# Attention layers of a four-layer block: the second selection cut into eight steps, its round moved to fourth place, and GpSimd given other weight chunks of q2b

## The chip, the cores and the metric

One core of one Trainium2 chip runs the whole program in one launch. The metric is device time in microseconds (us) of one execution. The kernel before takes 1843.88 us, the median of three runs (1841.74 to 1844.70). A difference of 0.2% is 3.7 us.

## The reference, cut to what matters

Sequence length 256, model width 1024, float32. Layers 0 and 1 (a gated delta rule, retention, pooling and a SwiGLU) are not touched. Layers 2 and 3 are attention layers, and each does this:

```python
(aq, ak, av, iq, ik, iw, bq, bk, bv, cq, ck, cv, gates) = split_columns(u @ w_in)
o_a = dsa_attention(qa, ka, av, iqr, ikr, iw * IDX_HEADS ** -0.5)   # 6 heads, keys chosen by top-k
o_b = dilated_attention(rope(bq), rope(bk), bv)                     # 12 heads in 3 groups
o_c = sink_window_attention(rope(cq), rope(ck), cv, sinks)          # 8 heads
merged = g0 * (o_a @ w_a) + g1 * (o_b @ w_b) + g2 * (o_c @ w_c)
return merged @ w_o
```

Branch a first scores every earlier token with eight small index heads, and each query keeps its 64 best keys:

```python
score = jnp.einsum('bqh,bqhs->bqs', iwb, relu(iq @ ik * idx_scale))
_, idx = lax.top_k(where(causal, score, -inf), 64)
```

## The kernel before, in words

**Weights.** Every projection streams through the core in chunks of 128x1024 float32 (512 KB): 568 of them. SyncE fetches chunk i into one of four slots of `raw` (line 560) as soon as the split of chunk i-4 has freed the slot. ScalarE rounds it to `whi` (line 654) once TensorE has used chunk i-4. VectorE or, for the chunks in the set `SHARED`, GpSimd subtracts to get the rest, `wlo` (lines 1144 and 1800; this is called the split of a chunk). TensorE then does 24 matmuls of 128x256 for a chunk: high weights by high inputs, high by low, low by high (line 2019).

**Order.** There is no scheduler. Each of the five engines has its own Python function that writes its queue in program order, and a generator yields after each chunk. `run(attention(index, attend), fill)` puts the attention pieces between chunks: each `yield 1` of `attention` lets the next chunk of `fill` through. In an attention layer `fill` is q2b (16 chunks, the queries and keys of branches b and c), gate0, gate1 (8 each), wa (3), gate2 (8), wb (2). A chunk of q2b is called by its number below; chunk 16 is the first of gate0. The split of chunk k+3 stands in the step of chunk k.

**Pieces of attention.** `index(half)` gives the scores and the selection for the queries of one half (0 or 1). TensorE does 16 small matmuls, ScalarE a Relu of them, VectorE adds eight weighted heads (line 1150), then does eight selection rounds, each a MAX (line 1662) and a MATCH_REPLACE (line 1664), and two instructions that make the mask. The second half has 256 columns, the first 128. Before the change VectorE does two selection rounds in one step.
`attend(x)` is one of ten rounds: scores on TensorE, mask and maximum on VectorE, exponentials on ScalarE, then transposes, values and a last transpose. A round takes three chunks. The order of the rounds is the list `kinds`; rounds 0 and 1 are branch a for both halves, then come four of b and four of c. Both selections are complete before round 0, which stands before chunk 12. Round t stands before chunk 12+3t.

**Rope.** A pair of q2b tiles is turned in four steps: VectorE evacuates the bank with two multiplications (to `products` for sin, to `QF` for cos) once both chunks of the pair are done; SyncE copies the sin product between partitions with four small DMAs (`exchange`, line 582), which stand in its queue behind the fetch of chunk 2(r-6)+9; GpSimd adds (`rope(r)`, line 1800). The eight pairs of q2b are r = 6 to 13. A round of branch b reads tiles of r = 6 to 11, so TensorE waits in front of the first b round for addition 11. Addition 11 stands in GpSimd's queue behind the split of chunk 17, exchange 11 in SyncE's queue behind the fetch of chunk 19, which waits for the split of chunk 15.

**Banks.** The pairs of q2b alternate between banks 6 and 7, so that chunk 10 needs the evacuation of the pair 6-7 (chunks 6 and 7, r = 9), chunk 12 that of 8-9, and so on.

Of the kernel before, what the change touches and what calls it, by code (L numbers as in the profile page):

```python
# [143 lines left out]
SHARED |= {312 + 138 * L + c for L in (0, 1) for c in chain((1, 2, 3, 8, 9, 10), range(12, 44, 2))}  # L144
# [130 lines left out]
def program(nc, ins, out):  # L275
    with ExitStack() as ctx:
# [251 lines left out]
        kinds = [("a", 0, 0, 3), ("a", 1, 0, 3), ("b", 0, 0, 3), ("b", 0, 1, 3), ("b", 1, 0, 3), ("b", 1, 1, 3),  # L528
# [3 lines left out]
        def attention(index, attend):  # L532

            yield from index(0)
            yield from index(1)
            before = None
            for x in rounds:
                g = attend(x)
                next(g)
                yield 1  # L540
                if before is not None:
                    next(before)
                yield 1
                next(g)
                if before is not None:
                    next(before)
                yield 1
                if before is not None:
                    next(before, None)
                before = g  # L550
            for _ in before:
                yield 1
# [77 lines left out]
        def scalar(a):  # L630
# [347 lines left out]
            def second(L):  # L978
# [37 lines left out]
                def index(half):  # L1016
# [10 lines left out]
                    for _ in range(6):  # L1027
                        yield 1
# [29 lines left out]
                def gates(name, steps, *at):  # L1058

                    for i, s in enumerate(steps):  # L1060
                        yield s
                        if i in at:
# [3 lines left out]
                             gates("wa", after_step(project("gate1", L), 5, lambda: branch_high("wa", L, *a_att.at("OO", L, 1))), 1, 3),  # L1066
# [75 lines left out]
        def vector(v):  # L1142
# [457 lines left out]
            def second(L):  # L1600
# [43 lines left out]
                def index(half):  # L1644
# [5 lines left out]
                    v.wait_ge(*a_att.at("rel", L, half, 1, 4 // (512 // nk) - 1))  # L1650
                    for c in range(2):
                        for j in range(4):
                            at = 8 * half + 2 * j + c
                            x = stt(here, rel[:, c, j, :], IW[:, at:at + 1], here if c + j else causal, OP.mult, OP.add)
                            if c + j < 4:
                                x.then_inc(*v_att.up())
                                v.wait_ge(*v_att.now())
                    x.then_inc(*v_att.up("score", L, half))
                    yield 1
                    for r in range(8):  # L1660
# [5 lines left out]
                        if r % 2:  # L1666
                            yield 1
# [130 lines left out]
        def gpsimd(g):  # L1798
# [156 lines left out]
            def second(L):  # L1955
# [20 lines left out]
                def index(half):  # L1976
                    for _ in range(6):
# [30 lines left out]
        def tensor(e):  # L2008
# [545 lines left out]
            def second(L):  # L2554
# [13 lines left out]
                def index(half):  # L2568
# [14 lines left out]
                    for _ in range(6):  # L2583
                        yield 1

                def attend(x):
# [4 lines left out]
                    if t == 2:  # L2591
# [299 lines left out]
```

## Time and profile before

| what | value |
|---|---|
| median of 3 runs | 1843.88 us |
| the profiled execution's own time | 1846.73 us |
| its span | 1844.9 us |
| TensorE busy | 1805.4 us, 98% |
| VectorE busy | 1250.9 us, 68% |
| ScalarE busy | 952.7 us, 52% |
| GpSimd busy | 315.0 us, 17% |
| granted TensorE clock, mean | 0.997 |

The page gives busy time by engine and by group of instructions. The view of waits lists what an engine waited for, in a stretch, with the total, the number of waits and the longest. A timeline gives for each instruction (or run of like ones, then with their count after the x) its start in us from the start of the span, its duration, engine, line, operation and tiles, and in square brackets the idle time before it and what ended it. When several instructions of one line follow without a pause they share one row, which shows the shape of the first only. "SPq" is the issue of DMAs by SyncE. The two attention layers are the same program; layer 2's attention part runs from 1032 to 1220 us, layer 3's from 1455 to 1650 us, and events of the one stand 423 us behind those of the other until the first wait of TensorE.

### The profile page before, as it was taken

How to read it: one execution, taken by the hardware profiler on the slowest of the kernel's cores; microseconds unless marked ns; L12 is line 12 of the kernel's file. 1: busy time of each engine (PE TensorE's matmuls, PEld its weight loads, DVE VectorE, ACT ScalarE, POOL GpSimd, SP SyncE). 2: the span in 40 equal slices, each digit the busy share in tenths (PEclk: the TensorE clock that was granted, in tenths of full speed). 3: DMA queues.
4: the chain of work that ended last, by engine and by line, in shares of the span. 5: the costliest groups of instructions: out<-in, count | busy, mean ns of one | idle time of the engine just before them, and what ended most of it. 6: DMA issues, size and time to landing. Idle time of an engine off the chain costs nothing.

```text
span 1844.9 us, 37214 instructions
## 1 busy us (share of the span) xinstructions
PE 1805.4 (98%) x15880; PEld 1714.5 (93%) x15880; DVE 1250.9 (68%) x1668; ACT 952.7 (52%) x1377; POOL 315.0 (17%) x174
## 2 busy tenths in 40 slices
PE   7999999999999999999999999999999999999998
PEld 7889998998888999999989999999999889999998
DVE  6885677665689648777648775587647795677643
ACT  5634466544554345564545445556534545556533
POOL 0050231000002303200001453320001352321000
PEclk9999999999999999999999999999999999999999
DMA  6453354656445334655665563456655654445663
GB/s 242 154 167 104 124 174 157 204 193 210 154 149 172 116 115 140 203 177 180 195 196 169 192 206 126 138 178 199 202 191 174 224 188 131 140 168 195 195 196 102
DMA packets 91524, 315.54 MB, mean 171 GB/s; under 512 B 11616, under 2 KB 12768, under 8 KB 91104
## 3 DMA queue, kind: packets, MB, share of 16 engines
q1 hardware_dynamic: 90784, 312.60, 52.3%
q8 instruction: 126, 2.06, 0.5%
q10 hardware_dynamic: 576, 0.57, 0.1%
q14 instruction: 38, 0.31, 0.1%
HBM read 302.90 MB, written 1.05 MB: 165 GB/s over the span
## 4 chain that ended last, share of the span: by engine, by line
PE 84%; DVE 12%; ACT 3%; issue 1%; DMA 0%; SPq 0%; DVEq 0%; ACTq 0%
PE bank L2019 82%; DVE wlo L1144 4%; DVE area L1144 3%; DVE area L1150 2%; ACT area L648 1%; ACT whi L654 1%; PE bank L2613 1%; DVE hl L1150 1%; DVE xT L1150 1%; DMA raw<-in_weights 0%; DVE area L1664 0%; DVE area L1662 0%; PE bank L2634 0%; PE bank L2253 0%; ACT L636 0%
## 5 line engine op out<-in xcount | busy, mean ns | idle before, releaser
L1144 DVE TENSOR_TENSOR wlo<-raw,whi 128x1024 fp32r<-128x1024 f32 x514 | 665.7, 1309 | 388.3 <-ACT whi L654 387.6
L2019 PE MATMUL bank<-hh,whi 128*128 128x256 f32 x2896 | 818.6, 284 | 23.8 <-DVE wlo L1144 18.7
L2019 PE MATMUL bank<-hh,wlo 128*128 128x256 f32 x2906 | 802.1, 277 | 0.0
L2019 PE MATMUL bank<-hl,whi 128*128 128x256 f32 x2896 | 794.4, 278 | 0.0
L654 ACT CAST whi<-raw 128x1024 fp32r<-128x1024 f32 x568 | 585.3, 1047 | 373.3 <-PE bank L2019 324.1
L2019 PEld LDWEIGHTS bank<-hh,whi 128*128 128x128 f32 x2896 | 545.6, 188 | 40.5 <-DVE wlo L1144 23.1
L2019 PEld LDWEIGHTS bank<-hh,wlo 128*128 128x128 f32 x2906 | 546.3, 188 | 0.0
L2019 PEld LDWEIGHTS bank<-hl,whi 128*128 128x128 f32 x2896 | 541.6, 189 | 1.5 <-issue 1.4
L1800 POOL TENSOR_TENSOR area<-area 128x512 f32<-128x512 f32 (+4 forms) x84 | 138.3, 1652 | 535.4 <-ACT area L648 213.3
L1800 POOL TENSOR_TENSOR wlo<-raw,whi 128x1024 fp32r<-128x1024 f32 x54 | 138.4, 2564 | 385.2 <-ACT whi L654 385.2
L2019 PE MATMUL bank<-FH,whi 128*128 128x256 f32 x640 | 177.4, 277 | 0.0
L2019 PE MATMUL bank<-FH,wlo 128*128 128x256 f32 x642 | 176.9, 276 | 0.0
L2019 PE MATMUL bank<-FL,whi 128*128 128x256 f32 x640 | 176.8, 276 | 0.0
L648 ACT ACTIVATE area<-area 128x256 f32<-128x256 f32 (+8 forms) x247 | 140.7, 579 | 50.3 <-DVE area L1144 17.4
L2019 PE MATMUL bank<-area 128*64 128x64 f32 (+6 forms) x2464 | 142.8, 248 | 6.6 <-DVE area L1144 5.2
L2019 PEld LDWEIGHTS bank<-area 128*64 128x64 f32 (+3 forms) x2464 | 122.6, 151 | 24.7 <-issue 7.0
L2019 PEld LDWEIGHTS bank<-FH,whi 128*128 128x128 f32 x640 | 120.2, 188 | 0.4 <-issue 0.3
L2019 PEld LDWEIGHTS bank<-FH,wlo 128*128 128x128 f32 x642 | 120.4, 188 | 0.0
L2019 PEld LDWEIGHTS bank<-FL,whi 128*128 128x128 f32 x640 | 120.2, 188 | 0.1
L1144 DVE TENSOR_TENSOR area<-bank,RSB 128x512 f32<-128x512 f32 (+1 forms) x118 | 80.0, 681 | 30.5 <-PE bank L2019 30.0
L1144 DVE TENSOR_TENSOR area<-bank,area 128x512 f32<-128x512 f32 (+3 forms) x140 | 81.6, 621 | 21.9 <-PE bank L2019 21.3
L2019 PE MATMUL bank<-wlo,FH 128*128 128x512 f32 x240 | 95.1, 396 | 0.0
(132 smaller groups left out, 1905.9 us busy)
## 6 DMA issues: line engine op xcount, KB each, us to landing
raw<-in_weights SPq DMA_DIRECT2D x568, 512.0 KB, 4.1
area<-area SPq DMA_DIRECT2D x100, 64.0 KB, 3.8
area<-area SPq DMA_DIRECT2D x16, 128.0 KB, 4.0
cst<-in_const SPq DMA_DIRECT2D x1, 1188.0 KB, 8.1
cst<-in_const SPq DMA_DIRECT2D x1, 1024.5 KB, 5.8
xT<-in_x SPq DMA_DIRECT2D x4, 256.0 KB, 7.3
out<-xT SPq DMA_DIRECT2D x4, 256.0 KB, 2.8
area<-in_lev SPq DMA_DIRECT2D x2, 384.0 KB, 6.9
```

The lines of the kernel that those rows point to most:

```text
L648: return a.activation(dst, src, fn, scale=scale, **more)
L654: a.copy(whi[:, i % RING, :], raw[:, i % RAW, :]).then_inc(*hi.up(i))
L1144: return v.tensor_tensor(dst, x, y, op)
L1150: return v.scalar_tensor_tensor(out=dst, in0=x, scalar=s, in1=y, op0=op0, op1=op1)
L1800: return g.tensor_tensor(dst, x, y, op)
L2019: return e.matmul(ps, x, y, start=start, stop=stop, skip_group_check=skip)
L2613: o = e.transpose(bank[b][:, 128 * u:128 * u + 128], x.grid()[:, j % 2, j // 2, 128 * kb:128 * kb + 128], C("eye"))
```

## The change

The index and attention parts of layers 2 and 3 are written in another order; no arithmetic changes.

1. The second selection (`index(1)`) is cut. Five of its steps stand before round 0, the others are taken one by one (`next(chosen)`) between the pieces of rounds 0 and 1. On VectorE each of its eight selection rounds has a step of its own, and the eight weighted heads are added in two steps of four, for both halves.
2. Each engine's `index` yields seven times in place of six. `index(1)`'s matmuls stand behind chunk 6 in place of chunk 5. Round 0 still stands before chunk 12.
3. The second round of branch a stands fourth: rounds 1 and 2 are now the first two of branch b. TensorE's wait for rope addition 11 is in front of round 1, and that of ScalarE's wa copy (in step 5 of gate1) is for the output of round 3.
4. Of q2b, GpSimd splits chunks 5, 6, 7, 12, 14 and 15 (before: 4, 5, 6, 11, 12, 13 and 15). From chunk 17 on nothing changes.

```diff
--- before.py
+++ after.py
@@ -141,7 +141,7 @@
 
 SHARED = {146 * L + c for L in (0, 1) for c in (51, 54, 57, 60, 63)}
 
-SHARED |= {312 + 138 * L + c for L in (0, 1) for c in chain((1, 2, 3, 8, 9, 10), range(12, 44, 2))}
+SHARED |= {312 + 138 * L + c for L in (0, 1) for c in chain((2, 3, 4, 9, 11), range(12, 44, 2))}
 
 
 class Signal:
@@ -525,25 +525,30 @@
             def grid(self):
                 return self.scores.rearrange("p (c n t) -> p c n t", c=2, t=self.nk)
 
-        kinds = [("a", 0, 0, 3), ("a", 1, 0, 3), ("b", 0, 0, 3), ("b", 0, 1, 3), ("b", 1, 0, 3), ("b", 1, 1, 3),
+        kinds = [("a", 0, 0, 3), ("b", 0, 0, 3), ("b", 0, 1, 3), ("a", 1, 0, 3), ("b", 1, 0, 3), ("b", 1, 1, 3),
                  ("c", 0, 0, 2), ("c", 0, 1, 2), ("c", 1, 0, 2), ("c", 1, 1, 2)]
         rounds = [Round(i, *x) for i, x in enumerate(kinds)]
 
         def attention(index, attend):
 
             yield from index(0)
-            yield from index(1)
+            chosen = index(1)
+            for _ in range(5):
+                yield next(chosen)
             before = None
             for x in rounds:
                 g = attend(x)
                 next(g)
+                next(chosen, None)
                 yield 1
                 if before is not None:
                     next(before)
+                next(chosen, None)
                 yield 1
                 next(g)
                 if before is not None:
                     next(before)
+                next(chosen, None)
                 yield 1
                 if before is not None:
                     next(before, None)
@@ -1024,7 +1029,7 @@
                             a.wait_ge(*e_att.at("index", L, half, c, k))
                             act(rel[:, c, k * per:k * per + per, :], bank[2 * c + k][:, 0:per * nk].rearrange("p (n t) -> p n t", t=nk), AF.Relu,
                                 scale=0.125 * 8.0 ** -0.5).then_inc(*a_att.up("rel", L, half, c, k))
-                    for _ in range(6):
+                    for _ in range(7):
                         yield 1
 
                 def attend(x):
@@ -1063,7 +1068,7 @@
                             gate(name, L, 2 * at.index(i))
 
                 fill = chain(project("q2b", L), project("gate0", L),
-                             gates("wa", after_step(project("gate1", L), 5, lambda: branch_high("wa", L, *a_att.at("OO", L, 1))), 1, 3),
+                             gates("wa", after_step(project("gate1", L), 5, lambda: branch_high("wa", L, *a_att.at("OO", L, 3))), 1, 3),
                              gates("wb", branch("wa", L), 0, 1),
                              after_step(project("gate2", L), 5, lambda: wb_high()),
                              gates("wc", branch("wb", L), 0, 1))
@@ -1647,23 +1652,24 @@
                     here, there = SC[:, 0:nk], SC[:, 256:256 + nk]
                     causal = C2(f"mA{half}")
                     v.wait_ge(*a_evac.at("v2b", L, 1))
-                    v.wait_ge(*a_att.at("rel", L, half, 1, 4 // (512 // nk) - 1))
                     for c in range(2):
+                        v.wait_ge(*a_att.at("rel", L, half, c, 4 // (512 // nk) - 1))
                         for j in range(4):
                             at = 8 * half + 2 * j + c
                             x = stt(here, rel[:, c, j, :], IW[:, at:at + 1], here if c + j else causal, OP.mult, OP.add)
                             if c + j < 4:
                                 x.then_inc(*v_att.up())
                                 v.wait_ge(*v_att.now())
-                    x.then_inc(*v_att.up("score", L, half))
-                    yield 1
+                        if c:
+                            x.then_inc(*v_att.up("score", L, half))
+                        yield 1
                     for r in range(8):
                         v.wait_ge(*v_att.now())
                         v.max(m8, here).then_inc(*v_att.up())
                         v.wait_ge(*v_att.now())
                         v.match_replace(there, m8, here, TAKEN).then_inc(*v_att.up())
                         here, there = there, here
-                        if r % 2:
+                        if half or r % 2:
                             yield 1
                     am = AM[:, 128 * half:128 * half + nk]
                     v.wait_ge(*v_att.now())
@@ -1974,7 +1980,7 @@
                 rest(after_step(project("v2b", L), 0, lambda: rope(5)))
 
                 def index(half):
-                    for _ in range(6):
+                    for _ in range(7):
                         yield 1
 
                 def attend(x):
@@ -2580,7 +2586,7 @@
                                 x = mm(bank[2 * c + k][:, nk * (j % per):nk * (j % per) + nk], QF3[r, 4 + j, qs], QF3[r, 8, 0:nk], True, True)
                                 if j == k * per + per - 1:
                                     x.then_inc(*e_att.up("index", L, half, c, k))
-                    for _ in range(6):
+                    for _ in range(7):
                         yield 1
 
                 def attend(x):
@@ -2588,7 +2594,7 @@
                     qs = slice(128 * x.half, 128 * x.half + 128)
                     if t == 0:
                         e.wait_ge(s_twin["ak"], 16 * (L - 1))
-                    if t == 2:
+                    if t == 1:
                         e.wait_ge(*g_rope.at("add", L, 11))
                     if t == 6:
                         e.wait_ge(*g_rope.at("add", L, 13))
```

On TensorE in layer 2, in front of the round that now reads q2b's tiles. Before, at chunk 15 (round 1, branch a), and three chunks on (round 2, branch b):

```order
L2019 MATMUL bank<-area 128x256 [waits att_act]
L2019 MATMUL bank<-area 128x256 [waits att_dve] x2
L2019 MATMUL bank<-area 128x256 x2
L2019 MATMUL bank<-area 128x256 [waits att_pe]
L2019 MATMUL bank<-hh,whi 128x256 [waits wlo_pool]
...
L2634 MATMUL bank<-cst,area 128x128 [waits att_act,att_dve]
L2019 MATMUL bank<-area 128x128 [waits att_dve,rope_pool]
```

The changed kernel at chunk 15:

```order
L2025 MATMUL bank<-hh,wlo 128x256
L2025 MATMUL bank<-area 128x128 [waits att_dve,rope_pool]
L2025 MATMUL bank<-area 128x128 [waits att_dve]
L2025 MATMUL bank<-area 128x128 x4
L2025 MATMUL bank<-hh,whi 128x256 [waits wlo_pool]
```

The wait on `rope_pool` (GpSimd's additions) stands three chunks earlier than before. On VectorE, layer 2, from the weighted heads of the second half to its fourth selection round. Before (the pairs MAX, MATCH_REPLACE are selection rounds, `proj` marks the evacuation of a bank, `whi` a split):

```order
L1150 SCALAR_TENSOR_TENSOR area<-area,cst 128x256 [waits att_act,evac_act]
L1150 SCALAR_TENSOR_TENSOR area<-area 128x256 [waits att_dve] x7
L1144 TENSOR_TENSOR wlo<-raw,whi 128x1024 [waits whi]
L1662 MAX area<-area 128x8 [waits att_dve]
L1664 MATCH_REPLACE area<-area 128x256 [waits att_dve]
L1662 MAX area<-area 128x8 [waits att_dve]
L1664 MATCH_REPLACE area<-area 128x256 [waits att_dve]
L1144 TENSOR_TENSOR wlo<-raw,whi 128x1024 [waits whi]
L1144 TENSOR_TENSOR area<-bank,area 128x512 [waits half1,proj]
```

The changed kernel:

```order
L1155 SCALAR_TENSOR_TENSOR area<-area,cst 128x256 [waits att_act,evac_act]
L1155 SCALAR_TENSOR_TENSOR area<-area 128x256 [waits att_dve] x3
L1149 TENSOR_TENSOR wlo<-raw,whi 128x1024 [waits whi,att_dve]
L1149 TENSOR_TENSOR area<-bank,area 128x512 [waits half1,proj]
L1149 TENSOR_TENSOR area<-bank,area 128x512
L1155 SCALAR_TENSOR_TENSOR area<-area 128x256 [waits att_act]
L1155 SCALAR_TENSOR_TENSOR area<-area 128x256 [waits att_dve] x3
L1149 TENSOR_TENSOR wlo<-raw,whi 128x1024 [waits whi]
L1668 MAX area<-area 128x8 [waits att_dve]
L1670 MATCH_REPLACE area<-area 128x256 [waits att_dve]
L1149 TENSOR_TENSOR area<-bank,area 128x512 [waits half2,proj]
```

The evacuation of the pair 6-7 (`half1`) stood behind eight heads and two selection rounds; it now stands behind four heads. On GpSimd, layer 2, from rope addition 7 (`half3`) to addition 9 (`half1`; `wlo` rows are splits). Before, then the changed kernel:

```order
L1800 TENSOR_TENSOR area<-area 128x512 [waits evac_dve,half3]
L1800 TENSOR_TENSOR wlo<-raw,whi 128x1024 [waits whi] x2
L1800 TENSOR_TENSOR area<-area 128x512 [waits evac_dve,half0]
L1800 TENSOR_TENSOR wlo<-raw,whi 128x1024 [waits whi]
L1800 TENSOR_TENSOR area<-area 128x512 [waits evac_dve,half1]
```

```order
L1806 TENSOR_TENSOR area<-area 128x512 [waits evac_dve,half3]
L1806 TENSOR_TENSOR wlo<-raw,whi 128x1024 [waits whi]
L1806 TENSOR_TENSOR area<-area 128x512 [waits evac_dve,half0]
L1806 TENSOR_TENSOR wlo<-raw,whi 128x1024 [waits whi]
L1806 TENSOR_TENSOR area<-area 128x512 [waits evac_dve,half1]
```

The two splits between additions 7 and 8 (chunks 11 and 12) become one (chunk 12), and the next is that of chunk 14 in place of 13.

## Rows read from the trace of the kernel before

**Rows 1.** The page, parts 1 and 5: TensorE whole, VectorE weight subtractions.
```profile
PE 1805.4 (98%) x15880; PEld 1714.5 (93%) x15880; DVE 1250.9 (68%) x1668; ACT 952.7 (52%) x1377; POOL 315.0 (17%) x174
...
L1144 DVE TENSOR_TENSOR wlo<-raw,whi 128x1024 fp32r<-128x1024 f32 x514 | 665.7, 1309 | 388.3 <-ACT whi L654 387.6
```

**Rows 2.** TensorE's waits, 1000:1240: engine, line <- releaser: total, times, longest us.
```profile
PE bank L2019 <- DVE area L1144: 1.1, 1, 1.1
```

**Rows 3.** TensorE's waits, 1420:1660, layer 3's attention.
```profile
PE bank L2019 <- DVE area L1144: 2.5, 2, 1.6
PE bank L2019 <- DVE wlo L1144: 2.0, 1, 2.0
```

**Rows 4.** Windows: length, busy us of PE, PEld, DVE, ACT, POOL, then clock, DMA.
```profile
1040.00:1090.00 50.00, 48.87 (x437) 47.10 (x436) 46.49 (x97) 23.33 (x46) 31.59 (x16) 1.00 0.63 203
1460.00:1515.00 55.00, 50.51 (x448) 48.45 (x447) 53.24 (x98) 22.85 (x41) 30.33 (x15) 1.00 0.54 176
```

**Rows 5.** TensorE timeline (start us, us, instruction): first and last matmul, q2b chunks 0 to 5.
```profile
1456.35 0.38 PE L2019 MATMUL bank<-hh,whi 128*128 128x256 f32 x1
...
1472.68 0.28 PE L2019 MATMUL bank<-hh,wlo 128*128 128x256 f32 x1
```

**Rows 6.** VectorE timeline, layer 2: two selection rounds; evacuation 10; end of round 0.
```profile
1059.55 0.42 DVE L1662 MAX8 area<-area 128x8 f32<-128x256 f32 x1
...
1060.53 0.43 DVE L1662 MAX8 area<-area 128x8 f32<-128x256 f32 x1
...
1075.09 2.21 DVE L1144 TENSOR_TENSOR area<-bank,area 128x512 f32<-128x512 f32 x4
...
1078.31 0.17 DVE L1147 TENSOR_SCALAR area<-area 128x6 f32<-128x6 f32 x1
```

**Rows 7.** VectorE timeline: two operations beside GpSimd ones.
```profile
1094.74 0.95 DVE L1147 TENSOR_SCALAR area<-area 128x2 f32<-128x2 f32 x1
...
1482.05 3.42 DVE L1144 TENSOR_TENSOR wlo<-raw,whi 128x1024 fp32r<-128x1024 f32 x1
```

**Rows 8.** GpSimd timeline, both layers: rope additions (area) and splits (wlo).
```profile
1054.84 1.29 POOL L1800 TENSOR_TENSOR area<-area 128x512 f32<-128x512 f32 x1 [1.82 <-DMA area<-area]
...
1071.45 2.63 POOL L1800 TENSOR_TENSOR wlo<-raw,whi 128x1024 fp32r<-128x1024 f32 x1 [0.91 <-ACT whi L654]
...
1084.32 1.28 POOL L1800 TENSOR_TENSOR area<-area 128x512 f32<-128x512 f32 x1
...
1093.26 2.40 POOL L1800 TENSOR_TENSOR wlo<-raw,whi 128x1024 fp32r<-128x1024 f32 x1 [2.83 <-ACT whi L654]
...
1482.01 2.38 POOL L1800 TENSOR_TENSOR wlo<-raw,whi 128x1024 fp32r<-128x1024 f32 x1 [2.25 <-ACT whi L654]
...
1496.08 1.28 POOL L1800 TENSOR_TENSOR area<-area 128x512 f32<-128x512 f32 x1 [2.02 <-DMA area<-area]
```

**Rows 9.** ScalarE timeline, layer 2: casts of chunk 15 and chunks 17, 18.
```profile
1070.32 1.05 ACT L654 CAST whi<-raw 128x1024 fp32r<-128x1024 f32 x1 [1.78 <-PE bank L2019]
...
1080.85 1.98 ACT L654 CAST whi<-raw 128x1024 fp32r<-128x1024 f32 x2
```

**Rows 10.** TensorE timeline, layer 2: scores of the second round.
```profile
1079.70 1.57 PE L2019 MATMUL bank<-area 64*128 64x256 f32 x12
```

**Rows 11.** SyncE queue's issues: raw is a chunk's weights, area a rope exchange.
```profile
1050.73 2.41 SPq L582 DMA_DIRECT2D area<-area  x4
...
1075.19 0.81 SPq L560 DMA_DIRECT2D raw<-in_weights  x2
...
1489.74 2.41 SPq L582 DMA_DIRECT2D area<-area  x4
```

**Rows 12.** The granted clock: after a 2.58 us pause, and around a 2.0 us one.
```profile
113.03 0.37 PE L2019 MATMUL bank<-area 64*64 64x64 f32 x2 [2.58 <-DVE area L1144]
...
112.00:116.00 4.00, 2.96 (x35) 2.68 (x36) 4.00 (x6) 0.00 (x0) 3.86 (x3) 0.59 0.45 125
1484.00:1488.00 4.00, 2.47 (x21) 2.47 (x22) 3.90 (x8) 0.65 (x1) 3.38 (x2) 1.00 0.31 101
```

## The prediction, written before the changed kernel was run

> **What bounds the kernel now.** I read the page first. TensorE is busy 1805.4 us, 98% of the span [rows 1], so what a change of order can return is TensorE's idle time, not anybody's work. The second view is the list of TensorE's waits in the two attention parts. In layer 2 it names one wait of 1.1 us for VectorE [rows 2], in layer 3 two on an evacuated bank of 2.5 us together and one of 2.0 us on a split [rows 3]. All four lie between chunks 9 and 14 of q2b. The third view, windows, says why: from 1040 to 1090 us VectorE is busy 46.49 of 50 us, in layer 3's stretch 53.24 of 55 [rows 4]. There VectorE is the engine that TensorE waits for. The sum returnable is 1.1 + 2.5 + 2.0 = **5.6 us**, 0.3% of the kernel.
>
> That layer 3 loses four times what layer 2 does, with the same program, is read in the timelines. VectorE's split of 1482.05 took 3.42 us [rows 7] in place of the mean 1.31 [rows 1]; GpSimd had begun a split at 1482.01 that ended at 1484.39 [rows 8], and 1.1 us of work was left then. So where both engines want such an operation, the one that is 40 ns late stands still until the other ends. The Trainium skill says this too (SBUF — State Buffer, Who interferes with whom): DVE operations with two SBUF inputs, and those in a 2-port mode such as a `tensor_scalar`, exclude GpSimd for a whole instruction, while one-input operations outside these modes don't. By that rule the trace agrees: a TENSOR_SCALAR of 2 elements took 0.95 us [rows 7] under a GpSimd split of 1093.26 to 1095.66 [rows 8], where a lone one took 0.17 [rows 6].
>
> **What goes.** A selection round of the second half takes 1060.53 - 1059.55 = 0.98 us [rows 6]. Before chunk 12 VectorE did eight of them, now three; 5 x 0.98 = 4.9 us leave, and the two mask instructions with them. Against that it makes one split more in this stretch, chunk 13 and 11 for 14, 1.3 us [rows 1]. So it is relieved of 3.6 us or more, and the evacuation that chunk 10 waited for stands behind four heads and no selection. VectorE was late by 1.1 us in layer 2 and by 2.0 + 1.6 in layer 3 [rows 2, 3]. I count all 5.6 us as returned. If the collision of layer 3 repeats in a new place some stays: from 0 to 2.0 us. The cover for the selection rounds that now stand beside rounds 0 and 1 is the slack behind chunk 12, where VectorE's next splits are needed a chunk or more later.
>
> **What comes.** TensorE's wait for rope addition 11 moves from round 2 to round 1, three chunks earlier. The chain that leads to addition 11 does not move with it. I take as zero the moment in which ScalarE sees chunk 11 ended, 1070.32 in layer 2 [rows 9]. TensorE then does round 0's scores and chunks 12 to 14, and is in front of round 1 at 1079.70 [rows 10]: **+9.4 us**, in both kernels.
>
> First path, through ScalarE. VectorE evacuates and does round 0's masks and maximum: from 1075.09 to 1078.48, 3.4 us [rows 6]. From there six exponentials, the casts, GpSimd's split of chunk 17 and addition 11, which ends at 1084.32 + 1.28 = 1085.60 [rows 8], take 7.1 us. Sum: +10.5, so **1.1 us late** at the least. With it comes the lock: GpSimd's split of chunk 15 now runs when the maximum's last TENSOR_SCALAR is due, and 0.8 to 1.3 us are added by the measure of the 0.95 us row [rows 7]: +11.3 to +11.8.
>
> Second path, through the queues. The cast of chunk 15 and its split begin at 1071.45 - 1070.32 = +1.1 [rows 8, 9]. But GpSimd must now first do chunk 14's split, which cannot begin before chunk 10's end plus a cast. A chunk is (1472.68 - 1456.35) / 143 x 24 = 2.74 us [rows 5]; so that is -2.7 + 1.1 = -1.6, with 2.4 us of split to +0.8, addition 9 to +2.1, and chunk 15's split to **+4.5** [2.4 and 1.3 us, rows 8]. SyncE then issues one fetch (0.4 us) [rows 11] and exchange 11 at about +5.0. From the issue of an exchange to the addition that waited for it I find 1054.84 - 1050.73 = 4.1 us at the low end and 1496.08 - 1489.74 = 6.3 at the high end [rows 8, 11]. Addition 11 ends between 5.0 + 4.1 + 1.3 = +10.4 and +12.6.
>
> The later of both gives +11.8, typically, if VectorE is in time: a wait of **2.4 us**. If the split of chunk 11 on VectorE falls behind GpSimd's split of chunk 12, which I estimate to begin within half a microsecond of each other (GpSimd's at -3 x 2.74 + 1.1 = -7.1), VectorE is up to 2.4 us late, chunk 15's fetch with it, then addition 9 and all that follows: about 1.6 us more, a wait of **4.0 us**. I give both the same weight and take 3.2 us for each layer, 6.4 us for two, with bounds of 1.1 us (only the first path, no lock) and 5.6 us (slow split and slowest landing) for each. Behind this wait nothing new is late: while TensorE stands, all the others catch up.
>
> **The clock.** Behind a pause of 2.58 us the granted clock was 0.59 over 4 us [rows 12], so about 0.41 x 2 x 4 = 3.3 us at 1.2 GHz. Behind the 2.0 us pause it stayed 1.00 [rows 12]. Dense matmuls in 3.3 us at half clock lose 1.6 us. A wait of 2.4 us may escape this, one of 4.0 hardly; I count one of the two layers, 1.6 us. The Trainium skill (TensorE: Matmul & The Clock Gate, What's actually happening) has the same two levels, with the lower one after idleness; by it, too, a longer pause costs more than its length.
>
> **Other edits.** The wa copy of ScalarE waits for round 3's output, written after chunk 26 and wanted in step 5 of gate1, chunk 29: three chunks of cover, 8 us. The seven yields move `index(1)`'s matmuls one chunk and add none. Two b rounds in front of a's second move work only.
>
> **The sum.** -5.6 + 6.4 + 1.6 = **+2.4 us**. The profiled execution (1846.73 us, 1.8 above its span) stands 2.85 above the median of the runs. I put the change on the median: 1843.9 + 2.4 = **1846.3 us**. It is smaller than the 0.2%, 3.7 us, that a measurement of this kernel can tell from no change.
>
> **Rivals.**
> *The exchange is early and addition 11 in time.* If landings are at their low end and the lock falls well, the wait is under 0.6 us in each layer: -5.6 + 1.2 = -4.4, and at best -5.6, 1838.3 to 1839.5 us. For it speaks that VectorE's relief is surely there; against it that the first path alone needs 10.5 of 9.4 us. Chance 0.18.
> *One long wait in each layer.* Place: TensorE in front of round 1. Price: 5.6 us each and 1.6 us of clock each: -5.6 + 11.2 + 3.2 = +8.8, 1852.7 us. It decides from a wait of about 3.9 us per layer, where with the clock the loss passes 3.7 us (-5.6 + 7.8 + 1.6 = +3.8). For it speaks the near tie between the splits of chunks 11 and 12. Chance of a loss between 3.7 and 8.8: 0.32.
> *The change moves the waits without removing them*, since VectorE loses the race against GpSimd elsewhere: 2.0 us stay, and with waits of 1.1 to 2.4 us the total is -1.4 to +1.2, 1842.5 to 1845.1. It looks like no change. Chance 0.12.
>
> **How the numbers follow.** My forecast, 2.4 to 4.0 us per layer and the clock in none, one or both, spans -5.6 + 4.8 = -0.8 to -5.6 + 8.0 + 3.2 = +5.6: 1843.1 to 1849.5. What of it stays within 3.7 us has chance 0.38; its upper end is counted with the long wait. With the third rival that makes 0.50 for no telling change. Faster 0.18, slower 0.32. The range reaches into the first rival and to most of the second: 1838.8 to 1850.6.
>
> **What would show it.** In the changed profile the waits on VectorE of chunks 9 to 14 are gone; TensorE has one wait per layer, at a row `bank<-area` of 128 columns, released by GpSimd's addition; the row before addition 11 is a GpSimd split that itself waited for ScalarE, or the addition waited for the DMA. Windows there show a clock below 1.00. I am wrong if TensorE reaches round 1 without a wait of over 1 us, or if VectorE still delays chunk 10 or 12.

## The result, and the profile of the changed kernel

| | kernel before | changed kernel |
|---|---|---|
| median of the runs | 1843.85 us (1841.74 to 1844.70, 4 runs) | 1849.91 us (1849.09 to 1853.18, 4 runs) |
| profiled execution, its span | 1846.73, 1844.9 us | 1853.18, 1851.4 us |
| mean granted clock of TensorE | 0.997 | 0.993 |

The changed kernel is slower: ratio 1.0040, 95% interval 1.0027 to 1.0052, that is +7.4 us (+5.0 to +9.6); the medians alone differ by 6.1. The forecast was 1846.3 us and no telling change, the range up to 1850.6. The median lies in the range; the sign was the rival's that I had called *one long wait in each layer*.

TensorE's waits in the two attention parts, 1000:1240 and then 1420:1665 us, as in [rows 2, 3]:

```profile
PE bank L2025 <- POOL area L1806: 4.6, 1, 4.6
PE bank L2025 <- DVE wlo L1149: 0.8, 1, 0.8
...
PE bank L2025 <- POOL area L1806: 5.4, 1, 5.4
PE bank L2025 <- DVE wlo L1149: 1.2, 1, 1.2
```

The new wait is there once a layer, in front of round 1, released by GpSimd's addition 11. Two short waits for ScalarE of 0.4 to 0.6 us stand in every kernel and are left out here and in the sums. Of the old waits of 5.6 us, 2.0 us stayed, as waits for VectorE's split of chunk 11. Idle time went from 5.6 to 12.0 us (0.8 + 4.6 + 1.2 + 5.4).

The page, part 1, beside [rows 1]:

```profile
PE 1805.5 (98%) x15880; PEld 1715.0 (93%) x15880; DVE 1249.2 (67%) x1670; ACT 952.4 (51%) x1377; POOL 303.5 (16%) x172
```

Windows, columns as in [rows 4]: the two stretches of that group, then the 4 us slices at the two long waits.

```profile
1040.00:1090.00 50.00, 44.60 (x378) 43.01 (x378) 38.97 (x76) 20.14 (x36) 22.55 (x13) 0.93 0.61 182
1460.00:1515.00 55.00, 48.47 (x411) 47.01 (x410) 43.76 (x92) 22.04 (x34) 25.95 (x13) 0.94 0.60 186
...
1080.00:1084.00 4.00, 4.00 (x24) 3.78 (x25) 2.38 (x5) 0.00 (x0) 0.00 (x0) 0.50 0.29 92
1084.00:1088.00 4.00, 4.00 (x31) 4.00 (x31) 3.48 (x8) 1.27 (x3) 0.00 (x0) 0.83 0.24 71
...
1508.00:1512.00 4.00, 1.41 (x12) 1.36 (x12) 0.00 (x0) 0.00 (x0) 1.35 (x2) 0.58 0.81 261
1512.00:1516.00 4.00, 4.00 (x24) 3.83 (x21) 3.59 (x8) 0.00 (x0) 0.00 (x0) 0.57 0.01 2
```

VectorE is 38.97 us of 50 busy, not 46.49, but most of that difference is the time in which it, too, stands while TensorE waits. Over the 39 us that begin 8 us behind the part's first scores (they are defined below) and end before the long wait, it was busy 35.25 us in place of 37.50 in layer 2 and 34.43 in place of 37.75 in layer 3: relieved of 2.3 and 3.3 us, for the 3.6 or more of the forecast. And the clock fell to its lower level at both waits (0.50, and 0.58 and 0.57). TensorE's busy time in the page grew by 0.1 us only and hides this; the next paragraph says what makes up for it.

**Measuring by parts.** In each trace I therefore take the part from the first scores of the first selection to a wait of 0.55 us that every kernel has near the attention's end. TensorE's timeline, the two marks of layer 2 in the kernel before and in the changed one:

```profile
1032.22 1.16 PE L2019 MATMUL bank<-area 64*128 64x128 f32 x16 [0.40 <-ACT area L648]
1187.20 1.06 PE L2613 MATMUL bank<-cst,area 128*128 128x128 f32 x8 [0.55 <-ACT area L1055]
```
```profile
1028.20 1.16 PE L2025 MATMUL bank<-area 64*128 64x128 f32 x16 [0.40 <-ACT area L653]
1189.87 0.84 PE L2619 MATMUL bank<-cst,area 128*128 128x128 f32 x6 [0.55 <-ACT area L1060]
```

That is 154.98 us before and 161.67 after in layer 2; the same marks of layer 3 give 158.62 and 162.09. Together **+10.2 us**: waits +6.4, and a rest of 3.8 that I put down to the clock and test below. Between the parts lie 267.9 to 268.3 us in all fourteen traces of this study, behind them to the end of the span 230.9 to 231.3. What stands in front of the first part is the same program everywhere and took 1023.7 to 1033.9 us, another value in each trace (here 4.0 us less in the changed kernel's, with the same number of matmuls: TensorE was busy 1003.6 us in it and not 1007.7, which hides the clock's cost in the busy time). That is noise enough for +10.2 in one pair of traces and +7.4 in the runs to stand together. Below, parts carry the argument, ratios check it.

**How addition 11 came to be late.** Layer 2 of the changed kernel; VectorE, GpSimd and SyncE's queue (start, us):

```profile
1056.28 4.06 DVE L1155 SCALAR_TENSOR_TENSOR area<-area 128x256 f32<-128x256 f32 x4
1060.26 2.31 DVE L1149 TENSOR_TENSOR wlo<-raw,whi 128x1024 fp32r<-128x1024 f32 x1
```
```profile
1057.58 2.46 POOL L1806 TENSOR_TENSOR wlo<-raw,whi 128x1024 fp32r<-128x1024 f32 x1 [5.53 <-ACT whi L659]
1060.02 1.47 POOL L1806 TENSOR_TENSOR area<-area 128x512 f32<-128x512 f32 x1
...
1068.31 2.40 POOL L1806 TENSOR_TENSOR wlo<-raw,whi 128x1024 fp32r<-128x1024 f32 x1
1073.98 1.29 POOL L1806 TENSOR_TENSOR area<-area 128x512 f32<-128x512 f32 x1 [3.27 <-DMA area<-area]
1075.24 2.35 POOL L1806 TENSOR_TENSOR wlo<-raw,whi 128x1024 fp32r<-128x1024 f32 x1
1078.52 1.26 POOL L1806 TENSOR_TENSOR area<-area 128x512 f32<-128x512 f32 x1 [0.93 <-DMA area<-area]
```
```profile
1067.07 2.42 SPq L587 DMA_DIRECT2D area<-area  x4
1069.54 1.53 SPq L565 DMA_DIRECT2D raw<-in_weights  x2
1071.17 2.82 SPq L587 DMA_DIRECT2D area<-area  x4
```

VectorE came late to chunk 11 in two steps. Four weighted heads took 4.06 us beside GpSimd's split of chunk 12 (4.98 in layer 3); then the split of chunk 11 started at 1060.26, behind GpSimd's addition of 1060.02, and took 2.31 us where others take 1.2 (in layer 3 it took 1.21). The second fetch in SyncE's row of 1069.54 waits for GpSimd's split of chunk 15, which ends at 1070.71; only then goes exchange 11 (1071.17), and the addition that waits for it starts at 1078.52, 7.35 us later. In layer 3 it is 1501.95 to 1509.28, 7.33 us. TensorE had been in front of round 1 since 1079.83 - 4.58 = 1075.25 (its row is shown with e6 below).

### The profile page after: what moved, and what is told of

Read it like the earlier page. It is cut to its first block, busy times and chain, and to the rows that moved or that the text cites. A ratio compares the mean times of both kernels' runs of the same rounds, so it can differ in the third digit from the quotient of the medians.

```text
span 1851.4 us, 37216 instructions
## 1 busy us (share of the span) xinstructions
PE 1805.5 (98%) x15880; PEld 1715.0 (93%) x15880; DVE 1249.2 (67%) x1670; ACT 952.4 (51%) x1377; POOL 303.5 (16%) x172
## 4 chain that ended last, share of the span: by engine, by line
PE 83%; DVE 10%; ACT 3%; DMA 1%; issue 1%; POOL 0%; SPq 0%; DVEq 0%; ACTq 0%
PE bank L2025 82%; DVE wlo L1149 4%; DVE area L1149 3%; DVE area L1155 2%; ACT area L653 1%; ACT whi L659 1%; PE bank L2619 1%; DMA raw<-in_weights 1%; DMA area<-area 1%; DVE hl L1155 1%; DVE xT L1155 1%; SPq L587 0%; POOL wlo L1806 0%; PE bank L2640 0%; PE bank L2259 0%
## 5 line engine op out<-in xcount | busy, mean ns | idle before, releaser
L1806 POOL TENSOR_TENSOR wlo<-raw,whi 128x1024 fp32r<-128x1024 f32 x52 | 128.8, 2477 | 402.8 <-ACT whi L659 402.8
```

Of the source, the lines that this page charges most:

```text
L1806: return g.tensor_tensor(dst, x, y, op)
```

## The experiments

The runs were made in three groups, each on a chip of its own and with its own runs of the kernel before: e1, e2_busy_wait, e3 and e4 (kernel before 1840.4 us); c_after, e2_again, e5 and e6 (1841.8); e7 to e10 (1839.6). Waits and parts are from one trace each, "waits" being TensorE's for VectorE, then for GpSimd, in layers 2 and 3. How far to trust them: the changed kernel's two traces agree within 0.5 us in a part, those of e2 within 1.4. The ratios of one kernel from two groups can lie 0.3% apart (e2).

| kernel | waits, layer 2 | layer 3 | parts | ratio to before (95%) |
|---|---|---|---|---|
| before | 1.1 / 0 | 4.5 / 0 | 154.98, 158.62 | 1 |
| changed | 0.8 / 4.6 | 1.2 / 5.4 | 161.67, 162.09 | 1.0040 (1.0027 to 1.0052) |
| c_after (the same) | 1.0 / 5.4 | 1.3 / 4.9 | 161.67, 161.58 | 1.0034 (1.0016 to 1.0052) |
| e1_no_late_tile | 1.0 / 0 | 0 / 0 | 154.81, 153.69 | 0.9985 (0.9974 to 0.9996) |
| e2_busy_wait | 1.1 / 0.2 + filled | 0 / 1.5 + filled | 159.57, 158.81 | 1.0043 (1.0026 to 1.0059) |
| e2_again (the same) | 0.8 / 0.8 + filled | 0 / filled | 159.04, 157.38 | 1.0010 (0.9996 to 1.0023) |
| e3_tiles_in_order | 0 / 0 | 0 / 0 | 153.69, 153.70 | 0.9982 (0.9972 to 0.9992) |
| e4_old_splits | 1.7 / 4.5 | 2.9 / 4.8 | 162.53, 163.45 | 1.0087 (1.0073 to 1.0101) |
| e5_splits_alone | 2.7 / 0 | 3.3 / 0 | 156.99, 157.43 | 0.9998 (0.9984 to 1.0012) |
| e6_exchange_first | 1.2 / 1.7 | 1.1 / 2.0 | 156.21, 156.40 | 0.9985 (0.9970 to 1.0000) |
| e7_swap_11_12 | 0 / 5.4 | 0 / 5.7 | 161.15, 161.62 | 1.0054 (1.0036 to 1.0071) |
| e8_rounds_alone | 3.7 / 6.0 | 3.7 / 5.8 | 165.74, 165.29 | 1.0091 (1.0073 to 1.0109) |
| e9_exchange_alone | 1.2 / 3.8 | 0 / 4.7 | 161.19, 159.52 | 1.0050 (1.0034 to 1.0066) |
| e10_split17_alone | 1.2 / 4.2 | 1.1 / 5.2 | 160.21, 161.72 | 1.0062 (1.0044 to 1.0081) |

### Is it the wait for addition 11?

**e1_no_late_tile**, of the changed kernel:
```
-  "b": 17 + 2 * i + self.j
+  "b": 17 + (0 if self.turn == 1 else 2 * i) + self.j
-  if t == 1: e.wait_ge(*g_rope.at("add", L, 11))
+  if t in (1, 2): e.wait_ge(*g_rope.at("add", L, 9 if t == 1 else 11))
```

> Round 1's keys are all read from the pair of tile 17, so TensorE waits there for rope addition 9 alone, and for addition 11 only in front of round 2. Left out: the right logits of round 1 for its second and third group of heads; the number of instructions of every engine is that of the changed kernel. Theory A (the loss is TensorE's wait for addition 11 in front of round 1, with the clock behind it): the waits of 4.6 and 5.4 us go, with the clock's share, and the time falls by 10 to 12 us against the changed kernel, to 1838 to 1840 us, below the kernel before by 4 to 6. Rival B (addition 11 is late because VectorE and GpSimd are late as a whole, so that whoever comes next waits in its place): a wait of 3 us or more for addition 9 or for round 2 appears, and the time stays at 1847 us or above.

Measured 1836.65 us, and of the two long waits nothing is left. Parts fall by 6.9 and 8.4 us, and no other wait takes their place: theory A. The gain over the kernel before, 0.15% or 2.8 us, is below the 4 to 6 us expected, with an interval of 0.7 to 4.8 us. The parts are 5.1 us shorter than in the trace of the kernel before; why the runs show less stays open.

**e3_tiles_in_order** gets there with everything computed:
```
-  "b": 17 + 2 * i + self.j          # key tile
+  "b": 14 + i + 6 * self.j
-  "b": 11 + 2 * i + self.j          # query tile
+  "b": 11 + i + 6 * self.j
-  return tiles(np.concatenate([c("bq"), c("bk"), cq], 1))
+  b = [c(n, 128 * (2 * i + j), 128) for j in range(2) for n in ("bq", "bk") for i in range(3)]
+  return tiles(np.concatenate([*b, cq], 1))
   (the wait: round 1 for addition 8, round 2 for addition 11)
```

> The changed kernel with q2b's columns in another order: the three query tiles of round 1 and its three key tiles are the first six chunks (rope 11 to 16, of which round 1 wants additions 6 to 8), those of round 2 the next six (it waits for addition 11). Everything is computed. Theory A (the loss is that round 1 wants the last of twelve tiles): the wait in front of round 1 goes and nothing takes its place, since round 2 comes 3 chunks or 8 us later than addition 11's present end needs; 1837.5 to 1840.5 us. Rival B (VectorE and GpSimd are too late altogether, and the place of the wait decides nothing): 1847 us or more, with a wait for addition 8 or 11 in the rows.

1838.25 us, faster than the kernel before by 3.3 us (1.5 to 5.2) and than the changed one by more (1.0034 and 1.0040, from the other groups). Its list of TensorE's waits in 1000:1240, and in 1420:1660 the same two:

```profile
PE bank L2619 <- ACT area L1060: 0.6, 1, 0.6
PE bank L2025 <- ACT area L653: 0.4, 1, 0.4
```

Both parts take 153.7 us. The missing wait at chunk 11 looks like luck and not like the edit, which changes the order of no engine before round 1: a tie, taken up under e7, fell well in both layers here, and in layer 2 of e1 it did not. What the edit removes is the long wait. 153.7 us is the parts' length with no wait of this kind, and the other kernels' parts are this plus their waits plus the clock: before, layer 2, 153.7 + 1.1 = 154.8 for 154.98; e5, 153.7 + 2.7 = 156.4 for 156.99.

### What does the clock cost?

**e2_busy_wait**, and **e2_again** (the same kernel) beside **c_after** (the changed kernel):
```
   if t == 1:
+      ...                              # waits until bank 4 is free
+      for k in range(36):
+          mm(bank[4][:, 0:T], hh[:, k % 8, 0:128], hh[:, k % 8, :], True, True)
       e.wait_ge(*g_rope.at("add", L, 11))
```

> The changed kernel with 36 matmuls more (128x128 by 256 columns, results never read) in front of the wait for addition 11, so that TensorE works on while it waits. 36 of them at full clock fill about 36 x 0.11 = 4.0 us of the wait of 4.6 or 5.4, so nothing of the path is lengthened. If the lower clock behind the pause costs time of its own (my term: 1.6 us a time, now twice), the time falls by 2 to 3.5 us against the changed kernel, to 1846.5 to 1848, and the granted clock in the 12 us behind each wait is above 0.95. If the pause costs its length alone, the time stays at 1849.5 to 1851, whatever clock the rows show.

Six runs gave 1847.73 us, 1.0043 (1.0026 to 1.0059): against what I expected, no gain over the changed kernel's 1.0040, though the parts were shorter, 159.57 and 158.81 us. The changed kernel had not run on that chip, so both went together next, twelve runs each.

> The kernel with 36 matmuls in front of the wait, again, now timed on the same chip as the changed kernel. In its trace the stretch from TensorE's arrival in front of round 1 to the first matmul of the next chunk had 9.06 us in layer 2 (1077.06 to 1086.12) against 11.42 in the changed kernel's (1075.25 to 1086.67). If the lower clock costs time of its own, this kernel is 3 to 5 us faster than the changed one. If it costs nothing that is measured, the two are within 1.5 us.

> The changed kernel itself, beside the others on the same chip. By the first four runs' ratios (1.0040 on the chip of the result) it stands at 1.003 to 1.005 of the kernel before, 1846 to 1849 us if the kernel before stands at 1840.4 again, with one wait of 4 to 6 us in front of round 1 in each layer.

Now 1843.86 us (1842.01 to 1848.86) against 1848.97 (1845.38 to 1857.07): 5.1 us for the same order of work and TensorE kept busy. The windows of e2_again, where those of the changed kernel had 0.50:

```profile
1076.00:1080.00 4.00, 3.22 (x32) 3.01 (x32) 0.00 (x0) 0.00 (x0) 2.45 (x2) 1.00 0.90 272
1080.00:1084.00 4.00, 4.00 (x39) 3.88 (x36) 3.55 (x8) 0.31 (x1) 0.00 (x0) 1.00 0.18 56
```

From the end of addition 11 to the part's end take 107.4 and 107.8 us in e2_again, 110.1 and 109.8 in the changed kernel, 109.1 and 109.6 in c_after. So the lower clock costs 1.7 to 2.7 us behind each wait. Between the traces of c_after and e2_again the parts differ by 6.8 us, and only 3.6 of that lies behind addition 11; the other 3.2 is that addition 11 itself came sooner, most of it in layer 3, where the tie under e7 fell well. So not all of the 5.1 us of the runs need be the clock's. e2_busy_wait has 107.5 us behind addition 11 in both layers, so its trace agrees; its ratio does not, and 1.0043 and 1.0010 for one kernel, with intervals that don't meet, stay unexplained.

### Which part of the change does what?

**e5_splits_alone** (the kernel before, `SHARED` with the new list) and **e8_rounds_alone** (the kernel before, `kinds` in the new order, wa's copy behind round 3, `if t == 1` for the wait):

> The kernel before with the changed kernel's list of splits and nothing else of the change. In step 1 I had the new list relieve VectorE of nothing by itself (one split more for it). If the splits matter only together with the new rounds, the waits of 1.1, 2.5 and 2.0 us stay within 1.5 us of their sum and the ratio is 0.999 to 1.001. If the new list brings the gain by itself (no collision at chunk 11 or 12), it is 0.997 to 0.9985, 3 to 5.6 us less. If VectorE with one split more is later, 1.001 to 1.003.

> The kernel before with the order of rounds alone changed (the second a round stands fourth, wa's copy waits for round 3, and the wait for addition 11 is in front of round 1): all of the second selection is still done before the first round, and the splits are the old ones. Theory A (the selection's work in front of chunk 12 makes VectorE late, and all that feeds addition 11 with it; spreading it is worth something, but not the cost of the earlier wait): VectorE's waits of 1 to 2.5 us a layer stay and the wait for addition 11 is 4.5 us or more, parts of 163 to 166 us, ratio 1.006 to 1.011. Rival B (the spreading of the selection is what makes the wait, since rounds of selection now stand between VectorE's evacuations of chunks 12 to 17): this kernel is at or below the changed one, parts of 158 to 161 us, ratio 1.000 to 1.003.

e5: no difference that can be told, and VectorE's waits are 6.0 us in place of 5.6. They stand before other chunks now: the list moves the waits and doesn't remove them. e8: the longest parts, theory A, though VectorE's waits did not stay at 1 to 2.5 us a layer but grew to 3.7. Layer 2 of it:

```profile
PE bank L2019 <- POOL area L1800: 6.0, 1, 6.0
PE bank L2019 <- DVE wlo L1144: 2.1, 1, 2.1
PE bank L2019 <- DVE area L1144: 1.6, 1, 1.6
```

**e4_old_splits** (the changed kernel, `SHARED` with the old list):

> The changed kernel with the kernel before's list of splits on GpSimd: of the q2b chunks 4, 5, 6, 11, 12 and 13 in place of 5, 6, 7, 12 and 14. Theory A (what makes addition 11 late is VectorE's split of chunk 11 behind GpSimd's work, and five fetches then bunched in front of exchange 11): chunk 11 is on GpSimd, its split is not late, exchange 11 lands in 4 to 6 us instead of 7.3, and TensorE's wait in front of round 1 falls from 5 to 2 to 3.5 us a layer: 1843 to 1847 us. Rival B (GpSimd is the engine in front of addition 11, and one split more there delays it): the wait grows by 1 to 2.4 us a layer, 1851 to 1855 us. Rival C (the order of rounds alone sets the wait): 1849 to 1851 us.

Not A: chunk 11 is on GpSimd, and the wait for addition 11 is still 4.5 and 4.8 us. The time, 1855.96 us, is B's in direction, but that wait did not grow either; waits for VectorE's evacuation did. Here, and in e8, addition 11 stands right behind GpSimd's split of chunk 17, which had waited 5.1 to 5.6 us for ScalarE: these are kernels in which the first path of the forecast decides. From before to the changed kernel: rounds alone +10.8 and +6.7 us, then the spread selection (e8 to e4) -3.2 and -1.8, then the splits (e4 to changed) -0.9 and -1.4. The spreading returns 5.0 us of the 17.4 that the new place of the wait costs. What the splits return is not shown: two traces of one kernel differ as much, and the ratios, 1.0087 and 1.0040 from two chips, are 8.6 us apart where the parts are 2.2.

### What holds addition 11?

**e7_swap_11_12**: in `SHARED`, `(2, 3, 4, 9, 11)` becomes `(2, 3, 4, 8, 11)`.

> The changed kernel with one number of its list changed: GpSimd splits chunk 11 and VectorE chunk 12, not the other way round. My forecast priced the split of chunk 11 behind GpSimd's split of chunk 12 at 1.6 us a layer. If that pair of splits makes TensorE's wait in front of chunk 11 (0.8 to 1.3 us) and the late fetches, both go, and addition 11 ends 1 to 3 us earlier: attention parts of 156 to 160 us each in place of 161.7. If GpSimd, which here takes 2.4 us for a split where VectorE takes 1.2, is itself in front of addition 11, TensorE waits for chunk 11 all the same and the parts stay at 161 us or grow.

VectorE's wait at chunk 11 is gone in both layers:

```profile
PE bank L2025 <- POOL area L1806: 5.4, 1, 5.4
PE bank L2619 <- ACT area L1060: 0.6, 1, 0.6
```

but the wait for addition 11 grew, by 0.8 us in layer 2 and 0.3 in layer 3, and the parts are 161.15 and 161.62, only 0.5 us shorter each. More than half of what TensorE gains in front of chunk 11 it waits in front of round 1. So the long wait does not need a late split of chunk 11, to which my "1.6 us more" had tied its upper case. The late split is not free either, and e7 does not remove the collision: the four heads still take 3.9 us beside a split of GpSimd. In the changed order there is a tie between these heads and GpSimd's split of chunk 12. In layer 3 of e1, of both traces of e2 and of e9, and in both layers of e3, it fell the other way: heads 2.04 us, then a split of 3.42, and no wait at chunk 11. Within e2_again addition 11 then ended 2.1 us sooner, counted from the part's start, and within e9 0.6 us; both parts are 1.7 us shorter than their layer 2. No run sets the tie on purpose.

**e6_exchange_first**, **e9_exchange_alone** (first edit) and **e10_split17_alone** (second edit), of the changed kernel:
```
-  i = ... b0 + 2 * (r - 6) + 9
+  i = ... b0 + 2 * (r - 6) + 9 - 2 * (r == 11)
-  chain((2, 3, 4, 9, 11), range(12, 44, 2))
+  chain((2, 3, 4, 9, 11), range(12, 14, 2), range(16, 44, 2))
```

> The changed kernel with exchange 11 two fetches earlier in SyncE's queue, and with the split of chunk 17 on VectorE, so that nothing of GpSimd's stands between additions 10 and 11. If what holds addition 11 is the DMA queue (exchange 11 issued at +5.0 us and 7.3 us under way) it lands 1.5 to 3 us earlier and TensorE's wait falls from 4.6 and 5.4 to 2 to 3.5 us: 3 to 6 us less than the changed kernel with the clock's share, a ratio of 1.000 to 1.002. If addition 11 is held by VectorE's own work in front of the exchange, the wait stays above 4 us and the ratio at 1.003 or more.

> The changed kernel with exchange 11 two fetches earlier in SyncE's queue and nothing else; the split of chunk 17 stays on GpSimd between additions 10 and 11. If the queue does all of what the run with both showed (parts of 156.2 and 156.4 us in place of 161.7), the parts are 156 to 157 us here too. If GpSimd's split has a share, addition 11 ends with the split in front of it, 2.4 + 1.3 us behind addition 10: a wait of 3.5 to 4.5 us for it and parts of 158 to 161 us.

> The changed kernel with the split of chunk 17 on VectorE and nothing else; SyncE's queue is as in the changed kernel. Addition 11 waited 0.93 us for the DMA there, behind the split. If the landing of exchange 11 is the limit, the wait in front of round 1 falls by less than 1 us and the parts stay at 161 to 162 us. If the split was, it falls by 2 us or more, and the parts with it and the clock to 156 to 158 us.

Both edits together take 5.5 and 5.7 us off the parts; the first alone 0.5 and 2.6 (in layer 3 the tie fell well too), the second alone 1.5 and 0.4. The ratios show no gain at all for either alone, 1.0050 and 1.0062, on a chip where the changed kernel did not run; for both together it is 0.9985, better than the 1.000 to 1.002 that I expected. GpSimd in layer 2 of e9, in e10 and in e6:

```profile
1075.09 1.80 POOL L1806 TENSOR_TENSOR area<-area 128x512 f32<-128x512 f32 x1 [2.48 <-DMA area<-area]
1076.84 2.35 POOL L1806 TENSOR_TENSOR wlo<-raw,whi 128x1024 fp32r<-128x1024 f32 x1
1079.15 1.26 POOL L1806 TENSOR_TENSOR area<-area 128x512 f32<-128x512 f32 x1
```
```profile
1073.46 1.71 POOL L1806 TENSOR_TENSOR area<-area 128x512 f32<-128x512 f32 x1 [2.66 <-DMA area<-area]
1077.82 1.26 POOL L1806 TENSOR_TENSOR area<-area 128x512 f32<-128x512 f32 x1 [2.65 <-DMA area<-area]
```
```profile
1071.39 2.50 POOL L1806 TENSOR_TENSOR area<-area 128x512 f32<-128x512 f32 x2 [3.22 <-DMA area<-area]
```

In e9 exchange 11 is early, and addition 11 has no wait in its brackets: it stands behind the split. In e10 there is no split, and it waits 2.65 us for the DMA. Two holds lie side by side, 1 us apart, and each hides the other. In e6 additions 10 and 11 run back to back (in layer 3 with 0.49 us between them). TensorE's timeline there, and in the changed kernel:

```profile
1073.95 0.94 PE L2025 MATMUL bank<-area 64*128 64x128 f32 x12 [1.73 <-POOL area L1806]
```
```profile
1079.83 1.65 PE L2025 MATMUL bank<-area 64*128 64x128 f32 x12 [4.58 <-POOL area L1806]
```

The twelve scores take 0.94 us behind a wait of 1.73 and 1.65 behind one of 4.58: the clock went with the wait. The theory of the queue alone, which I held when I wrote these expectations, fell. e6 computes everything too and lies at 0.9985; e3 is as good, and removes the reason for the hurry rather than two of its links.

## Why the prediction was wrong

- **What bounds, and where:** right. TensorE's idle time in these two parts moved, and the clock behind it; e3, without the long wait, has both parts at 153.7 us.
- **"I count all 5.6 us as returned":** 3.6 were. 2.0 us stayed by the collision the text allowed for (0 to 2.0), in both layers and not in layer 3 alone. e7 shows that it can be had, and that about half of it, 1.1 us, is then lost again in front of round 1.
- **TensorE's arrival at +9.4 us:** right, it was +9.5. Chunk 11's last matmul ends at 1065.71, TensorE arrives at 1075.25.
- **First path, through ScalarE (+10.5 to +11.8):** not the one that decided, by 0.93 us, the time that addition 11 waited for the DMA behind GpSimd's split; e10 confirms it. But it was mis-sized as well. The split of chunk 17 ended at 1077.59, so by this path alone addition 11 would have ended at +13.1. It stood right behind addition 10, which had waited 3.27 us for its own exchange (issued at 1067.07, addition at 1073.98), and the forecast had no addition 10 in this path. It fits that e9, which helps exchange 11 alone, does so little.
- **Second path, the failed step.** Exchange 11 was issued 1071.17 - 1065.7 = +5.5, near my +5.0. But "4.1 us at the low end and 6.3 at the high end" from issue to addition measured 7.35 and 7.33 us. Part of it is the issue of the four pieces, 2.82 and 3.39 us in place of 2.41. The rest is their way: each landed 4.8 to 5.5 us behind its issue, against 2.2 to 3.1 in my low row and 4.1 to 4.5 in the high one. Windows between issue and addition tell the difference: of the kernel before, my low and my high row; of the changed one, exchange 11 in both layers; and of e6, where it landed in 5.2 us.

```profile
1050.70:1054.80 4.10, 4.10 (x37) 3.70 (x34) 3.82 (x7) 2.99 (x5) 2.32 (x1) 1.00 0.69 211
1489.70:1496.10 6.40, 5.95 (x50) 5.84 (x52) 6.09 (x19) 1.79 (x2) 3.68 (x3) 1.00 0.93 290
```
```profile
1071.17:1078.50 7.33, 4.08 (x35) 3.88 (x33) 4.64 (x12) 4.06 (x14) 3.60 (x2) 1.00 0.90 259
1501.95:1509.28 7.33, 3.29 (x30) 3.09 (x28) 4.59 (x12) 4.03 (x14) 3.81 (x3) 0.95 0.92 261
```
```profile
1066.90:1072.10 5.20, 5.20 (x47) 5.12 (x46) 4.99 (x12) 4.41 (x14) 1.98 (x2) 1.00 0.67 199
```

The share of the DMA engines in the last column but one is 0.69 and 0.67 where the way is short, 0.90 to 0.93 where it is long. No run changes the load of the DMA engines and nothing else, so that the load is the cause is argued, not shown. What is shown is the time: in all twelve attention parts in which exchange 11 has its place of the changed kernel and addition 11 waits for it (the changed kernel, c_after, e1, both e2, e7, e10) it is 6.1 to 7.9 us. My low row never applied, and the high one was 1 us short here. Addition 11 ended at 1079.78, +14.1 against at most +12.6. The waits were 4.6 and 5.4 us where I took 3.2, with 2.4 and 4.0 as the cases.
- **The two cases of 2.4 and 4.0 us, by a late split of chunk 11:** the late split came (I had it even), but the wait is as long without it: e7.
- **The clock, 1.6 us once:** it fell in both layers, for 3.8 us in the difference of the parts. The price of one was 1.7 to 2.7 us for my 1.6; "one of the two layers" failed with the longer waits.
- **Other edits at nothing:** right as far as can be told. No wait for wa's copy or the moved matmuls is in the lists of waits.
- **The sum:** -3.6 + 10.0 + 3.8 = +10.2 on the parts, for my -5.6 + 6.4 + 1.6 = +2.4. The rival *one long wait in each layer* had -5.6 + 11.2 + 3.2 = +8.8: its mechanism and its size, and a chance of 0.32 where the tie between two splits was made the condition. The condition was the wrong one (e7). What should have been weighed is that the earlier place of the wait takes three chunks of cover, 8 us, from a chain of which both paths already came out late, so that every further delay in it was a loss.

## What to carry to other kernels

When a wait moves forward and its chain does not, price the chain at its worst rows, not at the middle: here two links were slow at once, and behind waits of 4.6 to 5.4 us the lower clock added 1.7 to 2.7 us. If a chain stays late after the obvious link is shortened, look for a second hold beside it before giving the theory up, since here only both edits together showed it. Better still, ask which tile the consumer needs last: putting the columns in the order of need (e3) removed the long wait with no engine made faster.

## What the runs showed of the hardware that I had not expected

- The clock: behind waits for addition 11 of 1.7 and 2.0 us (e6) the stretch from the end of addition 11 to the part's end takes 107.5 us, as with TensorE kept busy (107.4 to 107.8), and the granted clock is 1.00. Behind waits of 3.8 to 6.0 us it takes 109.1 to 110.4. The cost does not grow with the wait in these traces: 109.1 to 109.4 behind 6.0 and 5.8 us (e8), 110.4 behind 3.8 (e9).
- The same program up to the first attention part took 1023.7 to 1033.9 us in fourteen traces, and differed by up to 8.7 us among kernels of one chip, while the two later stretches agreed within 0.5 us. It is not in TensorE's waits: its idle time there is 23.8 to 25.3 us in every trace, and its busy time is what differs, 998.4 to 1009.3 us. What stretches it stays open.
- An exchange of four pieces of 32 rows occupies SyncE's queue for 2.4 to 3.6 us, about as long as TensorE needs for a chunk (2.74 us); two of them in a row took 5.3 us (e6).
- Four weighted heads on VectorE, 128x256 each, take 2.04 us, and 3.9 to 5.1 us where a split of GpSimd runs beside them. Where that split began 0.7 to 1.4 us behind the first head they were slowed, where it began 1.7 us behind it they were not.
